# The two output projections with 1088 tokens cut 512, 512 and 64 instead of 364, 364 and 364

## The reference, cut to what matters

```
def delta_mixer(x, ...):                 # layer 0
    ...
    o = rmsnorm(o, o_norm) * jax.nn.silu(z.astype(jnp.float32))
    y = o.reshape(bsz, length, A_V_W).astype(x.dtype) @ w_out      # (tokens, 1024) @ (1024, 1024)
    return y, s_fin.astype(x.dtype), conv_new

def diff_mixer(x, ...):                  # layer 1
    ...
    o = rmsnorm(o, subln) * (1.0 - lam_init)
    return o.reshape(bsz, length, B_V_W).astype(x.dtype) @ w_out   # (tokens, 1024) @ (1024, 1024)

# in each layer:
    hp = hp + mp                         # prompt stream + projection
    hs = hs + ms                         # sample stream + projection
    hp = hp + mlp(hp, ln_mlp[layer], w_up[layer], w_down[layer])
    hs = hs + mlp(hs, ln_mlp[layer], w_up[layer], w_down[layer])
```

## Time and profile before

| | |
|---|---|
| device time, median of 2 runs | 3929.26 us (3925.35 and 3933.17) |
| span of the profiled execution, first to last instruction | 3928.0 us |
| the profiled execution's own time beyond its span | not given; the median of the runs is 1.3 us above the span |
| PE busy | 3667.4 us, 93% |
| PEld busy (weight loads, beside PE) | 3445.5 us, 88% |
| DVE, ACT, POOL busy | 1535.0, 1103.6, 787.2 us |
| first projection on PE | from 1283.5 us |
| second projection on PE | from 3037.3 us |
| mean granted clock of PE | 0.936 of full speed |

### The profile page before, as it was taken

The page is one execution under the profiler, slowest core; times in us unless marked ns, Lnnn a source line. Parts: engine busy times, 40 slices in busy tenths (PEclk is TensorE's granted clock), DMA queues, the critical chain, the costliest instruction groups (busy, mean ns, idle before and its releaser), DMA issues. The chain is left out here.

```text
span 3928.0 us, 55963 instructions
## 1 busy us (share of the span) xinstructions
PE 3667.4 (93%) x21703; PEld 3445.5 (88%) x21703; DVE 1535.0 (39%) x2331; ACT 1103.6 (28%) x1863; POOL 787.2 (20%) x477
## 2 busy tenths in 40 slices
PE   5888888888888999999999999999999999999998
PEld 5888878878877999999999788878887999999998
DVE  2534434544442722222224334444445723222223
ACT  2332332332342221111122333333344131111111
POOL 1303303303302132111112211110111231111110
PEclk8999999998997999999999888988888999999999
DMA  2000100110100111111111211111111111111111
GB/s 86 20 26 18 28 23 18 28 29 12 28 23 12 44 44 44 44 47 46 44 44 38 69 50 42 37 44 49 50 44 34 43 44 44 45 47 44 44 49 62
DMA packets 254674, 155.53 MB, mean 40 GB/s; under 512 B 9520, under 2 KB 251714, under 8 KB 254402
## 3 DMA queue, kind: packets, MB, share of 16 engines
q1 hardware_dynamic: 254426, 151.95, 13.1%
HBM read 133.49 MB, written 18.42 MB: 39 GB/s over the span
## 5 line engine op out<-in xcount | busy, mean ns | idle before, releaser
L210 PE MATMUL ps<-x_hi,w_hi 128*128 128x364 f32 x2880 | 694.9, 350 | 31.5 <-DVE conv_in_sample L1090 17.5
L210 PE MATMUL ps<-x_hi,w_lo 128*128 128x364 f32 x2880 | 644.8, 333 | 0.0
L210 PE MATMUL ps<-x_lo,w_hi 128*128 128x364 f32 x2880 | 644.3, 332 | 0.0
L210 PEld LDWEIGHTS ps<-x_hi,w_hi 128*128 128x128 f32 x2880 | 503.7, 192 | 70.0 <-issue 24.2
L210 PEld LDWEIGHTS ps<-x_lo,w_hi 128*128 128x128 f32 x2880 | 509.7, 191 | 0.0
L210 PEld LDWEIGHTS ps<-x_hi,w_lo 128*128 128x128 f32 x2880 | 509.3, 191 | 0.0
L200 DVE TENSOR_TENSOR w_lo<-w_raw,w_hi 128x1024 fp32r<-128x1024 f32 x200 | 282.7, 1414 | 508.6 <-ACT w_hi L196 508.5
L196 ACT ACTIVATE w_hi<-w_raw 128x1024 fp32r<-128x1024 f32 x200 | 211.8, 1059 | 832.4 <-PE ps L210 614.9
L190 POOL TENSOR_TENSOR w_raw<-w_raw,params 128x1024 f32<-128x1024 f32 x120 | 233.0, 1944 | 893.0 <-DMA w_raw<-in_w_in_a 409.5
L210 PE MATMUL ps<-hidden_hi,w_lo 128*128 128x364 f32 x1536 | 338.3, 328 | 0.0
L210 PE MATMUL ps<-hidden_lo,w_hi 128*128 128x364 f32 x1536 | 337.7, 328 | 0.0
(11 more groups left out here) (320 smaller groups left out, 5170.8 us busy)
## 6 DMA issues: line engine op xcount, KB each, us to landing
w_raw<-in_w_up SPq DMA_DIRECT2D x64, 512.0 KB, 3.9
w_raw<-in_w_down SPq DMA_DIRECT2D x64, 512.0 KB, 3.4
w_raw<-in_w_in_a SPq DMA_DIRECT2D x32, 512.0 KB, 4.0
w_raw<-in_w_kv SPq DMA_DIRECT2D x16, 512.0 KB, 3.8
cache_pages<-in_cache_k SPq DMA_DIRECT2D x128, 64.0 KB, 1.9
cache_pages<-in_cache_v SPq DMA_DIRECT2D x128, 64.0 KB, 1.9
x_in<-in_x_prompt SPq DMA_DIRECT2D x8, 512.0 KB, 4.1
state_sample<-in_state_delta SPq DMA_DIRECT2D x8, 512.0 KB, 4.0
```

Of the source, the lines that this page charges most:

```text
L210: mm = nc.tensor.matmul(PS[:, bank + g, 0:GRP], wt, x[:, k, g * GRP:(g + 1) * GRP], start=(k == 0 and t == 0), stop=(k == chunks - 1 and t ...
```

## The change

In the two output projections a new function, `split_products`, takes the place of `slab_products`. The number of matmuls stays at three a pair (k, t), their token ranges become 0 to 511, 512 to 1023 and 1024 to 1087, and the four columns of padding are no longer multiplied. A 512-column matmul fills its bank of PSUM. The eviction's first instruction becomes two, one over the two full banks and one over 64 columns of the third, the second of which releases `free`. Because the padding of `tmp` is now never written by it, two memsets set it to zero at the start of each projection. The other weight products keep their three times 364 columns.

```
+    SPLIT = ((0, 512), (512, 512), (SEQ, NS))
+
+    def split_products(s, bank, xh, xl, ks, chunks):
+
+        for k in ks:
+            for t, (w, x) in enumerate(((WH, xh), (WH, xl), (WL, xh))):
+                for g, (c, n) in enumerate(SPLIT):
+                    mm = nc.tensor.matmul(PS[:, bank + g, 0:n], w[s.slot][:, k, :], x[:, k, c:c + n],
+                                          start=(k == 0 and t == 0), stop=(k == chunks - 1 and t == 2))
         return mm
...
-                        mm = slab_products(n, 3 * s, OH, OL, [k], KC)
+                        mm = split_products(n, 3 * s, OH, OL, [k], KC)
...
+            for t in TMP:
+                nc.vector.memset(t[:, T:TP], 0.0)
             nc.vector.memset(SQA[:, :], 0.0).then_inc(self.zero.sem, 1)
...
-                    nc.vector.tensor_tensor(grouped(t), banks(3 * s), grouped(chunk(XH, m).bitcast(F32)),
-                                            ALU.add).then_inc(self.free.sem, 1)
+                    for a, n, b, g in ((0, SEQ, 3 * s, 2), (SEQ, NS, 3 * s + 2, 1)):
+                        ins = nc.vector.tensor_tensor(
+                            t[:, a:a + n].rearrange("p (g c) -> p g c", g=g), PS[:, b:b + g, 0:n // g],
+                            chunk(XH, m)[:, a:a + n].rearrange("p (g c) -> p g c", g=g).bitcast(F32), ALU.add)
+                    ins.then_inc(self.free.sem, 1)
```

More of the change, by code:

```diff
@@ L210, in slab_products @@
                     mm = nc.tensor.matmul(PS[:, bank + g, 0:GRP], wt, x[:, k, g * GRP:(g + 1) * GRP],
+                                          start=(k == 0 and t == 0), stop=(k == chunks - 1 and t == 2))
+        return mm
+    SPLIT = ((0, 512), (512, 512), (SEQ, NS))
[4 more added lines that the diff above has]
+                    mm = nc.tensor.matmul(PS[:, bank + g, 0:n], w[s.slot][:, k, :], x[:, k, c:c + n],
                                           start=(k == 0 and t == 0), stop=(k == chunks - 1 and t == 2))
```

## The result

The changed kernel takes 3959.66 us (two runs, 3959.11 and 3960.22) against 3929.26: a ratio of 1.008, 95% interval 1.0057 to 1.0103, so 30 us slower. The profiled execution has a span of 3957.9 us, 29.9 more than before.

A forecast was written before the change was run, and what follows sets the result against it. PE was taken to bound the projections: 24.7 us for longer triples plus 1.4 at 1.2 GHz less 0.6 for a wait that goes, 25.5 us on a span of 3928.0, gave 3955 us, range 3927 to 3972.

The forecast's parts named there:

- The term of the sum, 110 ns: Projections: the 64-column matmul costs 110 ns, as its weight load leaves the next 512 starting 110 ns later.
- The 512-column matmul: Projections: each takes 229 ns, between 213 and 235; two of them 457 ns of a 567 ns triple.
- the 15 ns over plain streaming: Projections before the change: 15 of a 364-column matmul's 167 ns are not plain streaming; taken as paid once a matmul.
- At 1.2 GHz: About five triples at each projection's start take 1.05 us against 0.91, 1.4 us more in all.
- The wait ahead of the MLP: PE's 0.3 us wait for `w_lo` before the MLP's first slab goes in both projections, 0.6 us back at most.
- Eviction and memsets: On DVE in the projections: eviction pieces of 1.22 and 0.22 us, 0.15 us longer together, and two memsets; all hidden.
- One sign: Changed profile of the projections: the next 512-column matmul starts 110 ns behind the 64-column one.
- the passes of L800: 16 passes of 8 columns at a granted clock of 1.00, 110 ns a pass, set by the weight load.
- the hidden load: Rival: PE takes the next weights' load early, so a projection triple is 499 ns, 3928 us; chance 0.11.
- two passes: Rival: fp32r of 64 columns runs as two passes with two loads, triple 677 ns, 3997 us; chance 0.07.
- the fallen clock: Rival: PE's clock falls to 1.2 GHz for good in the projections, 211 us more, 4140 us; chance 0.04.
- the 2 us that the prediction names: Hidden-load rival: by the skill's rule for a lone matmul the change would gain about 2 us.

The follow-up runs named there:

- evict_only: Kernel before (three times 364 columns) with the changed kernel's memsets and its eviction in two instructions, 728 and 360 columns; 3931.55 us, ratio 0.9996.

## Why the prediction was right, and where it was off

The forecast was 3955 us, the load of the narrow matmul uncovered; the time is 3959.66. The mechanism is shown by five runs that could have denied it: 192 columns cost what 64 do, 320 cost 36 ns more, 128 and 64 cost the same, 256 cost their stream and no more, and each 64-column matmul left out gives back 112 ns. The term of the sum, 110 ns, was right to 2 ns.

- *The 512-column matmul* was the term that was mis-sized: 229 ns was taken, with the 15 ns over plain streaming paid once a matmul; it is 232. From the triples, 320 columns are 611 - 463 = 148 ns and 256 are 497 - 232 - 148 = 117, so a column costs (232 - 117) / 256 = 0.45 ns and a matmul 2 ns beside. Most of the 15 ns grow with the columns after all, and the upper end, 235, was nearer. With the load's 2 ns this makes 575 for 567, 8 ns x 374 = 3.0 us.
- *At 1.2 GHz* a triple takes 1.07 us, not 1.05 (1286.57 to 1287.64): the load is 1.07 - 2 x 0.427 = 0.21 us. But fewer triples fall into the stretch at that clock: the first five take 4.95 us (1285.52 to 1290.47) where they took 4.61 (1283.52 to 1288.13), 0.3 us a projection more where 0.7 was reckoned.
- *The wait ahead of the MLP* of 0.3 us is gone, as said: its first matmul starts 0.58 us behind the start of the last triple, a triple's length.
- *Eviction and memsets* cost nothing (evict_only), and 1225 + 215 ns for the two pieces are the 1.22 + 0.22 us that were worked out.
- The projections lost 27.9 us for 25.5 predicted: 3.0 more by the triples and 0.7 less by the stretch at 1.2 GHz. The rest of the 4.7 us between forecast and time is the 2.0 us that came before the first projection, and scatter.
- *One sign was foretold wrongly*: that the next 512 would start 110 ns behind the 64. It starts 30 ns behind, and the delay is in its own length. Had one looked at that pair alone, the loss would have seemed to be in the 512. The rows of the kernel before had it already, and were misread: of the two passes of L1926, the one of 219 ns is the first, not the later one. Taken singly, as below, the second starts some 60 ns behind the first and L1927 110 ns behind the second, not the other way round. That the 110 ns read from this pair are right all the same is luck; the passes of L800 gave them without it.

```profile
2220.01 0.22 PE L1926 MATMUL ps<-k_roped,q_all_batches 128*128 128x64 f32 x1
...
2220.06 0.28 PE L1926 MATMUL ps<-k_roped,q_all_batches 128*128 128x64 f32 x1
2220.18 0.19 PE L1927 MATMUL ps<-sample_mask_bf,ident_bf 128*128 128x64 bf16 x1
```

- Of the rivals, the hidden load would have shown 499 ns, two passes 768 narrow records, the fallen clock values under 1.00; none did. In the fallen clock's working a fifth of 211 us is 42 us, 1.1% and not over 2%; nothing else hangs on it. By the rule of the Trainium skill ("TensorE: Matmul & The Clock Gate", Back-to-back issue gap) that a lone matmul costs its columns at 2.4 GHz and about 2.5 ns, the 64 columns are an estimated 29 ns. That is how their record is spaced (0.03 us), but not what they cost in a stream in which each matmul loads weights, 110 ns. By that rule the four columns of padding would have given an estimated 0.6 us, 1.2 with the wait that goes, and not the 2 us that the prediction names.
- *A rival that the prediction doesn't name*: the 110 ns could be the time that PE takes for any pair of a load and a matmul, not the load of these weights. No run was made for it, but the kernel before has eight transposes (L314) of a smaller shape, each a load of 64 x 128 and a matmul of 64 columns, at a granted clock of 1.00. All eight matmuls lie within 0.68 us, 85 ns each at most, so a pair has no floor of 110 ns whatever it holds. That the floor is the load's own is the reading that is left.

```profile
30.62 0.57 PEld L314 LDWEIGHTS ps<-ident,x_in 64*128 64x128 f32 x8 [0.88 <-issue]
30.65 0.68 PE L314 MATMUL ps<-ident,x_in 64*128 64x64 f32 x8 [0.72 <-DVE x_lo L390]
...
30.65:31.20 0.55, 0.55 (x8) 0.54 (x8) 0.05 (x1) 0.55 (x3) 0.00 (x0) 1.00 0.00 0
```

## What to carry to other kernels

Where each matmul loads its own weights, count the longer of stream and load for every piece; here a load is 110 ns, by estimate the stream of about 240 fp32r columns ((110 - 2) / 0.45; the runs show only that it lies between 192 and 256), and shorter pieces pay the difference in full. Splitting into full banks and a remainder that streams for less than a load is worse than equal pieces, and putting the remainder first didn't mend it; the splits whose pieces are all above the load's length were equally good (497 to 501 ns a triple). And look for the price one record behind the short matmul, or better in the spacing of whole groups.

## What the runs showed of the hardware that was not expected

An fp32r column costs 0.45 ns at a granted clock of 1.00 (232 ns for 512 columns, 117 for 256), where half of the 0.833 at 0.50 would be 0.417. The stages ahead of the first projection vary from run to run by up to 13 us in these profiles, as much as some of the splits are apart: its first matmul starts at 1281.8 us in the profile with 192 columns, at 1285.5 in the changed kernel and at 1294.7 with 320, with the same code ahead of it. That is why the splits were told apart by the spacing of evictions and not by the time of a run.
